# Two transformer blocks on one Trainium2 core: x and the first QKV slab as one array in four pieces, and the order of work around them

## The reference

```python
def rms_norm(x, g):
    xf = x.astype(jnp.float32)
    y = xf * lax.rsqrt(jnp.mean(xf * xf, axis=-1, keepdims=True) + EPS)
    return (y * g.astype(jnp.float32)).astype(x.dtype)
...
def mixer_a(h, w_qkv, q_gain, k_gain, w_o, cos, sin):
    B, S, _ = h.shape
    qkv = (h @ w_qkv).reshape(B, S, A_GROUPS, 3, A_HEADS, HEAD_DIM)
    nums, dens, mxs = [], [], []
    for g in range(A_GROUPS):
        dil = A_DILATIONS[g]
        radius = A_WINDOWS[g] // (2 * dil)
        q = partial_rope(rms_norm(qkv[:, :, g, 0], q_gain[g]), cos, sin)
        k = partial_rope(rms_norm(qkv[:, :, g, 1], k_gain[g]), cos, sin)
        v = qkv[:, :, g, 2]
...
def first_block(x, norm1, ...):
    h = x
    for i in range(DEPTH):
        y = rms_norm(h, norm1[i])
        if kind == 0:
            y = mixer_a(y, ...)
        elif kind == 1:
            y = mixer_b(y, ...)
        h = h + y
        h = h + mlp_sq_relu(rms_norm(h, norm2[i]), mlp_w1[i], mlp_w2[i])
    return h
```

## Time and profile before

| | us |
|---|---|
| median of three executions | 2213.7 |
| lowest, highest | 2213.14, 2215.66 |
| the profiled execution | 2214.28 |
| its span | 2212.5 |
| TensorE busy | 2077.4 |
| VectorE busy | 807.3 |
| ScalarE busy | 291.2 |

### The profile page before, as it was taken

One profiled execution on the slowest core, in us unless ns is written; L12 is line 12 of the kernel. 1 busy time (PEld: TensorE's weight loads), 2 busy tenths in 40 slices (PEclk: granted clock), 3 DMA queues, 4 the chain that ended last, 5 costly groups with the idle time before them and its releaser, 6 DMA issues.

```text
span 2212.5 us, 23363 instructions
## 1 busy us (share of the span) xinstructions
PE 2077.4 (94%) x9698; PEld 1290.8 (58%) x9698; DVE 807.3 (36%) x1717; ACT 291.2 (13%) x576; POOL 21.5 (1%) x28
## 2 busy tenths in 40 slices
PE   8999999999999999999999888879999999888888
PEld 5666668888888888767743333333657643333333
DVE  3444533455331455445442222221355432222122
ACT  1222321000100000123210000000224110000000
POOL 0000000000000000000000000000000000000000
PEclk9999999999999999999999999999999999999999
DMA  7333345787445587432489999999832689999997
GB/s 316 114 117 140 134 152 220 279 303 272 152 152 216 204 308 285 148 125 84 173 350 422 428 427 429 427 429 420 301 140 89 266 353 427 427 428 428 427 427 328
DMA packets 108596, 623.45 MB, mean 282 GB/s; under 512 B 6096, under 2 KB 8528, under 8 KB 73424
## 3 DMA queue, kind: packets, MB, share of 16 engines
q1 hardware_dynamic: 94816, 566.63, 63.9%
q0 software_dynamic: 12672, 50.33, 6.2%
q10 hardware_dynamic: 1008, 5.07, 0.6%
HBM read 620.96 MB, written 1.05 MB: 281 GB/s over the span
## 4 chain that ended last, share of the span: by engine, by line
PE 74%; DMA 22%; DVE 2%; ACT 1%; issue 1%; SPq 0%; DVEq 0%
PE ps L1948 15%; PE ps L2505 14%; PE ps L2023 11%; DMA ring<-in_w_up 11%; DMA ring<-in_w_gate 10%; PE ps L1985 10%; PE ps L2189 5%; PE ps L2537 3%; PE ps L2182 3%; PE ps L2339 2%; PE ps L2076 1%; PE ps L2517 1%; PE ps L2046 1%; PE ps L2066 1%; PE ps L2056 1%
## 5 line engine op out<-in xcount | busy, mean ns | idle before, releaser
L2505 PE MATMUL ps<-ring,hT 128*64 128x512 f32 x992 | 254.0, 658 | 93.1 <-DMA ring<-in_w_gate 52.6
L1948 PE MATMUL ps<-hT,ring 128*128 128x256 f32 x1408 | 309.8, 381 | 3.6 <-ACT tmp L757 2.4
L1948 PEld LDWEIGHTS ps<-hT,ring 128*128 128x128 f32 x1408 | 268.0, 191 | 41.8 <-issue 3.1
L2023 PE MATMUL ps<-ring,hT 128*128 128x384 f32 x768 | 257.9, 490 | 2.2 <-DMA ring<-in_a_wqkv 2.2
L2537 PE MATMUL ps<-ring,arena 128*64 128x512 f32 x1024 | 226.9, 595 | 10.7 <-ACT arena L1053 9.6
L2505 PEld LDWEIGHTS ps<-ring,hT 128*64 128x64 f32 x992 | 82.9, 150 | 255.7 <-issue 254.5
L2505 PE MATMUL ps<-ring,tmp 128*64 128x512 f32 x992 | 224.5, 592 | 1.3 <-DMA ring<-in_w_up 1.3
L1985 PE MATMUL ps<-arena,ring 128*128 128x256 f32 x1024 | 224.7, 379 | 0.0
L1985 PEld LDWEIGHTS ps<-arena,ring 128*128 128x128 f32 x1024 | 193.6, 189 | 28.0
L2023 PEld LDWEIGHTS ps<-ring,hT 128*128 128x128 f32 x768 | 143.1, 191 | 94.2 <-DMA ring<-in_a_wqkv 2.9
L1765 DVE TENSOR_SCALAR arena<-arena 128x512 f32<-128x512 f32 x32 | 13.7, 427 | 427.3 <-ACT arena L1049 427.3
(11 more groups left out here) (355 smaller groups left out, 1681.1 us busy)
## 6 DMA issues: line engine op xcount, KB each, us to landing
ring<-in_w_gate SPq DMA_DIRECT2D x44, 2048.0 KB, 18.1
ring<-in_w_up SPq DMA_DIRECT2D x44, 2048.0 KB, 19.1
ring<-in_w_down SPq DMA_DIRECT2D x44, 2048.0 KB, 19.1
ring<-in_mlp_w SPq DMA_DIRECT2D x32, 2048.0 KB, 9.0
arena<-in_w_mod POOLq DMA_DIRECT2D x24, 2048.0 KB, 9.9
ring<-in_w_up SPq DMA_DIRECT2D x40, 1024.0 KB, 9.5
ring<-in_w_down SPq DMA_DIRECT2D x40, 1024.0 KB, 10.4
ring<-in_a_wqkv SPq DMA_DIRECT2D x24, 1536.0 KB, 6.5
```

Source lines behind the costliest of these rows:

```text
L1948: e = te.matmul(out[:, j, :], w[:, k, c0 + 128 * j:c0 + 128 * j + 128], src[:, k, :], start=(k == order[0]), stop=(k == order[-1]))
L2023: e = te.matmul(bank(r)[:, 0:WIDTH_A], h3[:, k, r * P:(r + 1) * P], weights[:, k, :], start=(k == HEAD_ORDER[0]), stop=(k == HEAD_ORDER[-1]))
L2505: e = te.matmul(bank(b)[SB * h:SB * h + SB], xs(k)[:, col:col + SB], slabs.tile(m + h).rearrange("p (k n) -> p k n", k=KD)[:, k, :], start ...
```

## The change

x (in the permuted order) and slab 0 become one input array `x_by_residue` of 128 x 5120. It has four pieces of 1280 columns (5 KB per partition, 640 KB), each with two chunks of x and the same two chunks of slab 0, in the order (0, 2), (4, 6), (1, 3), (5, 7). The pieces lie near the end of the arena and no longer in `oT` and in ring slot 0. SP issues param_1, common, the four pieces, waits for the last piece, counts slot 0 as landed and issues slab 1. ACT squares the x part of each piece (into the chunks' places in `tmp`), and issues const_a behind the fourth square without a wait for a slab. DVE makes hT by pieces; mean and root of the sums move behind `gain_q(0, 0)` and `gain_q(0, 1)`. PE fills with two matmuls, adds both token halves piece by piece (`project_first`, banks 0 and 1), and makes the token sums behind them. ACT's wait for slab 2 with the issue of xT stays where it is.

```diff
--- before.py
+++ after.py
@@ -318,7 +318,10 @@
 
     take = carve()
     oT = take(KD * S).rearrange("p (k t) -> p k t", k=KD)
-    xp = oT
+    HEAD_PIECE = 2 * S + 2 * WIDTH_A
+    head_in = [arena[:, ARENA - 96 - (4 - p) * HEAD_PIECE:ARENA - 96 - (3 - p) * HEAD_PIECE] for p in range(4)]
+    head_x = [a[:, 0:2 * S].rearrange("p (k t) -> p k t", k=2) for a in head_in]
+    head_w = [a[:, 2 * S:HEAD_PIECE].rearrange("p (k n) -> p k n", k=2) for a in head_in]
     ca_c, ca_n = columns(CONST_A)
     const_a = take(ca_n)
     qkT = [take(GROUPS_A * 2 * S).rearrange("p (g i t) -> p g i t", g=GROUPS_A, i=2) for _ in range(2)]
@@ -604,12 +607,11 @@
             load(n, wrows(n), rows_of(w, r0), turns)
 
 
+        sp.dma_start(param_1[:, :], param_1_d).then_inc(consts_in, 16)
         sp.dma_start(common[:, :], common_d).then_inc(consts_in, 16)
-        sp.dma_start(param_1[:, :], param_1_d).then_inc(consts_in, 16)
         if first:
             for p in range(4):
-                sp.dma_start(xp[:, 2 * p:2 * p + 2, :].rearrange("p k t -> p (k t)"),
-                             xp_d[:, 512 * p:512 * p + 512]).then_inc(xp_in[p], 16)
+                sp.dma_start(head_in[p], xp_d[:, HEAD_PIECE * p:HEAD_PIECE * p + HEAD_PIECE]).then_inc(xp_in[p], 16)
 
         def mlp(n, w1, w2):
             load_cols(n, w1, 0)
@@ -624,9 +626,11 @@
             for c in range(KD):
                 for w in range(3):
                     n = A_QKV + 3 * c + w
-                    load(n, ring.tile(n)[:, 0:KD * WIDTH_A], a_wqkv[c, w])
                     if n == A_QKV:
-                        ring.wait_landed(sp, n)
+                        sp.wait_ge(xp_in[3], 16)
+                        sp.sem_inc(landed[n % SLOTS], 16)
+                    else:
+                        load(n, ring.tile(n)[:, 0:KD * WIDTH_A], a_wqkv[c, w])
             for s in range(2):
                 load_cols(A_WO + s, a_wo[0], 512 * s)
             mlp(MLP0, mlp_w1[0], mlp_w2[0])
@@ -783,9 +787,9 @@
         if first:
             for p in range(4):
                 act.wait_ge(xp_in[p], 16)
-                sc.activation(tmp[:, 512 * p:512 * p + 512], xp[:, 2 * p:2 * p + 2, :].rearrange("p k t -> p (k t)"),
-                              ACT.Square).then_inc(x_squared, 1)
-            ring.wait_landed(act, A_QKV)
+                k = HEAD_ORDER[2 * p]
+                sc.activation(tmp.rearrange("p (k t) -> p k t", k=KD)[:, k:k + 3:2, :], head_x[p], ACT.Square
+                              ).then_inc(x_squared, 1)
             act.dma_start(const_a[:, :], const_a_d).then_inc(const_a_in, 16)
             ring.wait_landed(act, A_QKV + 2)
             act.dma_start(xT, x_d).then_inc(x_in, 16)
@@ -1329,17 +1333,18 @@
                 fold(2 * l + 2, 3)
 
         if first:
-            for k in range(KD):
-                if k % 2 == 0:
-                    dve.wait_ge(xp_in[k // 2], 16)
-                e = ve.tensor_scalar(h3[:, k, :], xp[:, k, :], par1("norm1")[:, k:k + 1], None, ALU.mult)
-                if k % 2:
-                    e.then_inc(h_ready, 1)
-
-            token_mean(0, 7)
-            own.step(ve.tensor_scalar(tok_eps, tok_mean, DH * EPS, None, ALU.mult))
-            rsqrt(tok_root, tok_t, tok_mean)
-            dve.sem_inc(x_root, 1)
+            for p in range(4):
+                dve.wait_ge(xp_in[p], 16)
+                for m, k in enumerate(HEAD_ORDER[2 * p:2 * p + 2]):
+                    e = ve.tensor_scalar(h3[:, k, :], head_x[p][:, m, :], par1("norm1")[:, k:k + 1], None, ALU.mult)
+                e.then_inc(h_ready, 1)
+
+            def first_root():
+
+                token_mean(0, 7)
+                own.step(ve.tensor_scalar(tok_eps, tok_mean, DH * EPS, None, ALU.mult))
+                rsqrt(tok_root, tok_t, tok_mean)
+                dve.sem_inc(x_root, 1)
 
             def gain_q(c, b):
                 w, r = b // 2, b % 2
@@ -1394,6 +1399,8 @@
                     if c < KD:
                         gain_q(c, 2 * w)
                         gain_q(c, 2 * w + 1)
+                    if c == 0 and w == 0:
+                        first_root()
                     if c > 0:
                         mask(c - 1, 2 * w)
                         mask(c - 1, 2 * w + 1)
@@ -1922,8 +1929,8 @@
 
             t3 = tmp.rearrange("p (k t) -> p k t", k=KD)
             for k in range(KD):
-                if k % 2 == 0:
-                    pe.wait_ge(x_squared, k // 2 + 1)
+                if k == 0:
+                    pe.wait_ge(x_squared, 4)
                 for r in range(NT):
                     e = te.matmul(bank(b)[:, r:r + 1], t3[:, k, r * P:(r + 1) * P], com("ones")[:, 0:1],
                                   start=(k == 0 and r == 0), stop=(k == KD - 1), skip_group_check=True)
@@ -2008,6 +2015,17 @@
             down(NF - 1, n + MLP_SLABS - 1, pairs=True)
 
         if first:
+            def project_first():
+
+                for p in range(4):
+                    pe.wait_ge(h_ready, p + 1)
+                    for r in range(NT):
+                        for m, k in enumerate(HEAD_ORDER[2 * p:2 * p + 2]):
+                            e = te.matmul(bank(r)[:, 0:WIDTH_A], h3[:, k, r * P:(r + 1) * P], head_w[p][:, m, :],
+                                          start=(p == 0 and m == 0), stop=(p == 3 and m == 1))
+                        if p == 3:
+                            e.then_inc(slab_done if r else half_done, 1)
+
             def project(c, i):
                 w, r = i // 2, i % 2
                 slab, n = A_QKV + 3 * c + w, 6 * c + i
@@ -2018,8 +2036,6 @@
                     pe.wait_ge(q_gained, 4 * c + i - 1)
                 weights = wcols(slab, WIDTH_A)
                 for k in HEAD_ORDER:
-                    if n == 0 and k % 2 == 0:
-                        pe.wait_ge(h_ready, k // 2 + 1)
                     e = te.matmul(bank(r)[:, 0:WIDTH_A], h3[:, k, r * P:(r + 1) * P], weights[:, k, :],
                                   start=(k == HEAD_ORDER[0]), stop=(k == HEAD_ORDER[-1]))
                 e.then_inc(half_done if r == 0 else slab_done, 1)
@@ -2077,15 +2093,16 @@
                                   start=(k == 0 and o % 2 == 0), stop=False, skip_group_check=True)
                 return e
             early, last = range(KD - 1), (KD - 1,)
-            fill(6, 3)
+            fill(2, 3)
             for c in range(KD):
                 before = c > 0
-                project(c, 0)
                 if before:
+                    project(c, 0)
                     turn_q(c - 1, 3)
+                    project(c, 1)
                 else:
+                    project_first()
                     sums_first(7)
-                project(c, 1)
                 if before:
                     scores(c - 1, 0)
                 project(c, 2)
@@ -2738,8 +2755,11 @@
         i["router_w_2"].reshape(KD, P, E).transpose(1, 0, 2).reshape(P, -1),
         np.broadcast_to(i["router_b_2"], (P, E))], 1)
     feature_major = lambda a: a.T.reshape(KD, P, S).transpose(1, 0, 2).reshape(P, -1)
+    x_first = feature_major(x[order]).reshape(P, KD, S)
+    w_first = i["a_wqkv"][0].reshape(KD, P, GROUPS_A, 3, KD, P).transpose(4, 3, 1, 0, 2, 5)[0, 0].reshape(P, KD, WIDTH_A)
+    head = np.concatenate([a[:, HEAD_ORDER[2 * p:2 * p + 2], :].reshape(P, -1) for p in range(4) for a in (x_first, w_first)], 1)
     arrays = {
-        "x_t": feature_major(x), "x_by_residue": feature_major(x[order]),
+        "x_t": feature_major(x), "x_by_residue": head,
         "common": np.concatenate([common, by_partition(i["c_2"][0])], 1), "const_a": const_a, "const_2": const_2,
         "param_1": param_1, "param_2": np.stack(param_2), "param_r": param_r,
         "positions": np.concatenate([np.broadcast_to(i["positions_2"], (P, S)), i["positions_2"].reshape(NT, P).T], 1),
```

## The result

The changed kernel takes 2221.45 us (median of six executions, 2219.09 to 2223.23) against 2214.44 for the kernel before in the same measurement: ratio 1.0031, 95% interval 1.0018 to 1.0044. It is slower, by 7 us, where I forecast 0.8 us of gain. The profiled execution took 2219.97, its span 2218.1.

The account below looks back on a forecast made before the run. Projection (0,2) was taken to be gated by the square behind ScalarE's slab 2 wait: 25.3 + 5.16 + 1.7 = 32.2 against 32.96, so 0.8 us off the profiled 2214.28 gives 2213.5. Range 2210.4 to 2216.0.

Parts of the forecast that it names:

- What bounds the head: Before projection (0,2): bank 0 waits for the square behind ScalarE's slab 2 wait, released at 25.2; four us of idle.
- Pieces and landing: Input loads at the start: first piece landed at 6.9, last at 11.6 (between 11.4 and 12.1), slab 2 at 23.6.
- size rule of the Trainium skill: Input loads: at least 1 MiB per DMA, 341 GB/s for 1 MB alone; last piece then at 12.6, time 2213.9.
- the row of 373 GB/s: Input loads: traced rate of the stretch with most 2 KB rows, taken as the least for the remaining 1.99 MB, 5.3 us.
- Head, sums, clock: First projections 7.5 to 17.8, sums to 21.3; 3.4 us at half clock costs (0,2) 1.7 us, ending at 32.2.
- the root behind the gains: VectorE's root of the token sums, 2.4 us, moved behind gain_q(0,1): costs nothing, its reader having 3.5 us of slack.
- Fill of two for six: TensorE's start: fill ends at 6.2, not 9.7; at half clock the head costs 1.7 more, covered by the slab 2 wait.
- does it reach the end?: Behind 33 us: TensorE waits for nothing over 0.7 us in the attention, so a shift there moves everything behind it.
- The slower rival: Rival for (0,2) and (0,3) behind the idle: six us at half clock cost 3.0, giving 2214.5; chance 0.15.
- The whole 6.5 us: Rival at the head: bank 0 free at 21.3, so TensorE's whole own gain arrives, giving 2207.2; chance 0.05.
- slower by over 0.2%: Whole kernel: a time above 2218.1, for the tail of the head-without-clock rival and anything unseen; chance 0.03.

Follow-up runs that it names:

- squares-first run: Changed kernel with ScalarE's wait for slab 2 and the issue of xT moved behind the first two squares: 2216.53 us, ratio 1.0007 to the kernel before.
- pad of 32 waits: Changed kernel with 32 already met TensorE waits (sixteen instructions) added behind the fill: 2216.32 us, ratio 0.9996 to the kernel before.
- four one-column matmuls: Changed kernel with four unread one-column matmuls (sixteen records) added behind the fill of two: 2216.72 us, ratio 1.0002 to the kernel before.
- squares first with four one-column matmuls: Changed kernel with the first two squares ahead of the wait for slab 2, plus four unread one-column matmuls behind the fill: 2211.96 us, ratio 0.9990.
- that with 32 waits: Changed kernel with the first two squares ahead of the wait for slab 2, plus 32 already met TensorE waits: 2210.51 us, ratio 0.9974.

## Why the prediction was wrong

**What bounds the head: right.** The square behind ScalarE's wait for slab 2 was named as the gate; the idle of "four us" was 4.04, the squares-first run moved (0,2) by 4.0 us, and nothing but the square and the issue of xT had changed places.

**Pieces and landing: right within about a microsecond.** The first piece was in at 5.8 (forecast 6.9), the last at 11.6 (11.6). By the size rule of the Trainium skill ("DMA: Bandwidth & Descriptors", section Bandwidth) I had estimated 12.6 for the last. It didn't hold against pieces queued behind each other, whose landings are 1.55 us apart (10.02 and 11.57); the row of 373 GB/s was the better guide. xT was issued at 24.0, not 23.6: slab 2 came 12.4 and not 12.0 behind the last piece.

**Head, sums, clock: right.** 6.75 to 18.2 and 21.7 against 7.5, 17.8 and 21.3; both halves took 11.5 us and not 10.3, since the first weight loads still took 0.34 us. The granted clock was 0.50 from 22.4 to 29.2, 3.5 us of it under (0,2); forecast 3.4. (0,2) ended at 32.89, not 32.2: 0.4 from the later start (25.73, not 25.3), and 0.3 because it took 7.16 us and not 6.86. I had used the 5.16 us of a projection behind another; the one that starts from idle took 5.43. The gain of this stage was forecast as 0.8 and is 0.07; the root behind the gains cost nothing.

**The step that failed** is "Fill of two for six": I wrote that nothing reads these matmuls and that the wait for slab 2 covers whatever the missing ones covered. I costed their time and their clock, and not that they are sixteen instructions ahead of two taken branches. The cleanest run is the pad of 32 waits, whose head ends at the same 32.89: it puts 7.7 us on just this (1.0031 against 0.9996, times 2214; about 3.5 either way by the two intervals). What the runs showed in its place are the two second stops, with idles of 4.79 and 3.27 us in the changed kernel's trace, and the half clock behind them. The change by itself is worth nothing that can be measured (0.9987 to 1.0005). With it falls "does it reach the end?": a shift at 33 us does go through, as the squares-first run shows, but I concluded from it that nothing else could happen there. And the 3.34 us "issue" at 1510 were in the earlier trace rows; I read the row for the clock and passed over the releaser.

**The rivals.** None was this one. The slower rival (a long half clock behind the idle) didn't come: 3.5 us under work, not 6. The whole 6.5 us didn't arrive, for the reason given. The range ended at 2216.0, 5.5 us short, and the chance given to slower by over 0.2% was 0.03. That share had to cover what I did not see, and it was too little.

**What is shown and what is not.** Shown: the pauses' place follows the number of TensorE instructions ahead of the joins one for one, whatever they are; without the pauses the change is no slower than the kernel before. That the pause is the wait for the next block of instructions is shown by the packets of the instruction queue, their number and their times, in every trace. q8 carries no engine's name, so that the packets are TensorE's is inferred from these. Why the next block is asked for only at the join isn't shown.

Open: with the pads, the times of one kernel fall into two groups about 5 us apart (four one-column matmuls: 2211.2 to 2211.9 and 2215.5 to 2217.7; 32 waits: 2211.4 to 2212.4 and 2216.1 to 2217.7). Both profiled executions are of the lower group. The one of the squares first with four one-column matmuls is of its upper group, and can be laid beside that with 32 waits, of its lower one, with the same order of work. Its lag is 5.3 us at 33 us, 7.0 at 500 and 8.7 at 724, out of 9.7 at the end; the two steps of 1.7 go with stretches of 3.4 us at 0.50 from 375.0 and 716.3 that the other doesn't have. So half-clock stretches and the head make most of that difference, but these are two kernels and one execution of each; that they make the groups stays a guess.

## What to carry to other kernels

An edit that adds or removes instructions moves every branch behind it. Where a profile shows "issue" idle behind a taken branch, count the instructions from there to the next pause, and try an edit with a pad of waits that are met already (two of them make one instruction here) before its own time is judged. Try more than one length: here eight instructions made it no better (1.0034 and 1.0042 against 1.0031), sixteen cured it. A stage whose end is gated by one engine's queue order, as here a square behind a wait for another slab, gains nothing from a faster engine until that order is changed.

## What the runs showed of the hardware

- A second stop behind a taken branch, where the join lay at most thirteen instructions ahead of an edge: 4.8 to 5.0 us of idle at the first join and 3.3 to 4.4 at the second where a few matmuls lay between, against 3.2 to 3.7 us for the first stop, which comes in every kernel. If no matmul lies between, the two are 8.5 to 9.1 us in one piece.
- The jump itself: TensorE's record of the branch lasts 6.0 to 6.5 us at both joins in all fourteen traces. The views put the idle of the first stop down to "issue" at the first join, but at the second mostly to a DMA (3.53 <-DMA ring<-in_w_gate in the kernel before), though the branch's record spans most of it.
- The instruction queue reads packets of 16 KB (16384 bytes each in the trace); around the first join 1505.9, 1511.9 and 1518.1 us in the changed kernel, 1507.3 and 1513.5 in the kernel before. They come 6 us apart with either.
- Sixteen waits on one engine made eight instructions, 32 made sixteen.
